# Fifteen more tiles turned by VectorE in 32x32 blocks and carried by small transfers, in a two-block transformer kernel in float32

## What is computed

```python
def first_block(x, mem, ...):
    for i in range(2):
        if i == 1:
            sk1, sk2, sv = shared_kv(x, kv_norm, w_kv, k_norm, cos, sin)
        u = rms_norm(x, mix_norm[i]) @ w_in[i]
        ...                                   # pooling (i = 0) or differential attention (i = 1)
        mem_out = memory_cross_attention(mem_q, mem, ...)
        x = x + concatenate([token_out, mem_out]) @ w_out[i]
        x = x + squared_relu_mlp(rms_norm(x, ffn_norm[i]), w_ff1[i], w_ff2[i])
    return x
# second block
#   u = rms_norm(x) @ w_in_2, split in eight parts; recurrence and attention on them
#   merged = sigmoid(m1) * (lru @ w_proj_a) + sigmoid(m2) * (att @ w_proj_b)
#   x = x + rms_norm(merged @ w_out_2) * norm_post
```

## Time and profile before

| | us |
|---|---|
| median of 3 runs | 3058.63 |
| lowest and highest | 3057.3, 3058.84 |
| the profiled execution, its own time | 3060.36 |
| its span | 3058.6 |
| PE busy in it | 3002.9 |
| ACT, DVE, POOL busy | 1504.9, 1793.7, 239.2 |

### The profile page before, as it was taken

One profiled execution on the slowest core, in us unless ns is written; L12 is line 12 of the kernel. 1 busy time (PEld: TensorE's weight loads), 2 busy tenths in 40 slices (PEclk: granted clock), 3 DMA queues, 4 the chain that ended last, 5 costly groups with the idle time before them and its releaser, 6 DMA issues.

```text
span 3058.6 us, 37252 instructions
## 1 busy us (share of the span) xinstructions
PE 3002.9 (98%) x13708; PEld 2484.1 (81%) x13708; DVE 1793.7 (59%) x2382; ACT 1504.9 (49%) x2019; POOL 239.2 (8%) x465
## 2 busy tenths in 40 slices
PE   8999999999999999999999999999999999999998
PEld 7877888888888778778888888888888888787886
DVE  6535655555455776866545555555546567786554
ACT  6534434444344555654434344444445547785433
POOL 0000302112030000001203021120000000010000
PEclk9999999999999999999999999999999999999999
DMA  7535666666675555546666666665665555666664
GB/s 258 183 113 178 214 200 199 205 192 210 188 227 187 165 167 156 166 146 197 202 201 204 200 198 206 192 206 206 203 199 186 157 166 172 192 205 202 225 240 152
DMA packets 313433, 586.12 MB, mean 192 GB/s; under 512 B 24784, under 2 KB 49744, under 8 KB 312528
## 3 DMA queue, kind: packets, MB, share of 16 engines
q1 hardware_dynamic: 293248, 541.13, 56.4%
q0 software_dynamic: 19472, 42.24, 4.3%
q10 hardware_dynamic: 576, 0.94, 0.1%
HBM read 561.15 MB, written 10.49 MB: 187 GB/s over the span
## 4 chain that ended last, share of the span: by engine, by line
PE 84%; DVE 8%; ACT 6%; issue 2%; DMA 0%; ACTq 0%; DVEq 0%
PE acc L1741 26%; PE acc L1743 26%; PE acc L1742 26%; ACT whi L909 2%; DVE wlo L1222 2%; PE tp L1759 1%; DVE wlo L1217 1%; ACT prob L1132 1%; PE sd L1822 1%; PE sd L1804 1%; PE sd L1910 1%; ACT qk L1140 0%; ACT whi L912 0%; ACT L1132 0%; PE sd L1900 0%
## 5 line engine op out<-in xcount | busy, mean ns | idle before, releaser
L1741 PE MATMUL acc<-whi,set_hi 128*128 128x512 f32 x4096 | 1618.6, 395 | 24.4 <-DVE wlo L1222 15.5
L1743 PE MATMUL acc<-whi,set_lo 128*128 128x512 f32 x4096 | 1597.4, 390 | 0.0
L1742 PE MATMUL acc<-wlo,set_hi 128*128 128x512 f32 x4096 | 1596.5, 390 | 0.0
L1222 DVE TENSOR_TENSOR wlo<-raw,whi 128x1024 fp32r<-128x1024 f32 x944 | 1131.9, 1221 | 683.9 <-ACT whi L909 682.9
L909 ACT ACTIVATE whi<-raw 128x1024 fp32r<-128x1024 f32 x944 | 975.3, 1057 | 764.2 <-PE acc L1743 622.1
L1741 PEld LDWEIGHTS acc<-whi,set_hi 128*128 128x128 f32 x4096 | 770.6, 188 | 197.6 <-DVE wlo L1222 24.6
L1743 PEld LDWEIGHTS acc<-whi,set_lo 128*128 128x128 f32 x4096 | 770.1, 188 | 163.0
L1742 PEld LDWEIGHTS acc<-wlo,set_hi 128*128 128x128 f32 x4096 | 771.0, 188 | 155.0
L875 POOL DMA_DIRECT2D u<-u x384 | 188.2, 498 | 1509.2 <-DVE u L1336 1474.1
L1217 DVE SCALAR_TENSOR_TENSOR wlo<-raw,par,whi 128x512 fp32r<-128x512 f32 x160 | 111.9, 748 | 52.6 <-ACT whi L912 51.8
L912 ACT ACTIVATE whi<-raw,par 128x512 fp32r<-128x512 f32 x160 | 103.8, 715 | 18.0 <-DMA raw<-in_w_kv 8.1
(11 more groups left out here) (233 smaller groups left out, 1240.5 us busy)
## 6 DMA issues: line engine op xcount, KB each, us to landing
raw<-in_w_ff SPq DMA_DIRECT2D x512, 512.0 KB, 4.6
raw<-in_w_in SPq DMA_DIRECT2D x248, 512.0 KB, 4.2
raw<-in_w_out SPq DMA_DIRECT2D x96, 512.0 KB, 4.3
raw<-in_w_mem_kv SPq DMA_DIRECT2D x32, 512.0 KB, 4.6
raw<-in_w_proj_a SPq DMA_DIRECT2D x32, 512.0 KB, 4.4
raw<-in_w_proj_b SPq DMA_DIRECT2D x32, 512.0 KB, 5.5
u<-u POOLq DMA_DIRECT2D x384, 32.0 KB, 4.9
raw<-in_w_kv SPq DMA_DIRECT2D x48, 256.0 KB, 3.3
```

Source lines behind the costliest of these rows:

```text
L1222: V.tensor_tensor(wlo[:, c], raw[:, c], whi[:, c].bitcast(f32), ALU.subtract).then_inc(w_lo, 1)
L1741: T.matmul(o, h[:, tok], whi[:, c], start=first, stop=False)
L1742: T.matmul(o, h[:, tok], wlo[:, c], start=False, stop=False)
L1743: ins = T.matmul(o, l[:, tok], whi[:, c], start=False, stop=last)
```

## The change

Fifteen tiles go from `tail` to `turned`: the first three of the four in both output projections, at the end of both feed-forward parts, and of the merged product in the second block. The fourth of each stays with PE.

- `turned`, `turn` and `shuffle` take a `room`: "u0" and "u1" are two pairs of areas in `u`, "kv" a pair in `kv`. (The plan's other names of rooms are not used by any tile.)
- POOL waits, ahead of the transfers of every turned tile, until all transfers of the earlier ones have landed.
- Where a norm's weights belong to the tile (`ffn0`, `ffn1`, and `pre` at the end of the second feed-forward part), ACT multiplies the turned tile by them in place, in four instructions on 128x256, waits for the last of them (`link`), and then copies it to `set_hi` in one of 128x1024. At the end of the first feed-forward part and in the merged product there are no weights, and the copy alone stands.
- The groups that read these tiles wait for the second tile before slab 0, for the third before slab 4, for the fourth before slab 6 (`fed_late`). The first group of the last product still waits for three tiles before slab 0.

```diff
-    def turned(self, slab_turn, slab_split, source, dst, kt, gain=None):
+    def turned(self, slab_turn, slab_split, source, dst, kt, gain=None, room="u0"):
...
+    def fed_late(self, g):
+
+        for k, left in ((0, 2), (NSLAB - 4, 1), (NSLAB - 2, 0)):
+            self.groups[g].need[k] = [("tail_lo", self.tails - left)]
...
             e = sc.end(g)
             sc.epilogue(g, "add", GW * i)
             sc.at("act", e + 1, "x_stat", rst_ffn, i, g)
-            sc.tail(e + 3, e + 5, ("x", i, g), dst, 4 * i, f"ffn{layer}")
+            if i < 3:
+                sc.turned(e + 1, e + 9, ("x", i, g), dst, 4 * i, f"ffn{layer}", room=f"u{i % 2}")
+            else:
+                sc.tail(e + 3, e + 5, ("x", i, g), dst, 4 * i, f"ffn{layer}")
...
             sc.epilogue(g, "add", GW * i)
             sc.at("act", S * (g + 1) + 1, "x_stat", next_rst, i, g)
             fs.append(g)
         for i, g in enumerate(fs):
-            sc.tail(S * (g + 1) + 3, S * (g + 1) + 5, ("x", i, g), a, 4 * i, next_gain)
+            if i < 3:
+                sc.turned(S * (g + 1) + 1, S * (g + 2) + 1, ("x", i, g), a, 4 * i, next_gain)
+            else:
+                sc.tail(S * (g + 1) + 3, S * (g + 1) + 5, ("x", i, g), a, 4 * i, next_gain)
...
         sc.epilogue(b, "proj_b", sc.tails)
-        sc.tail(S * (b + 1) + 3, S * (b + 1) + 5, ("out", b), 0, 4 * i)
+        if i < 3:
+            sc.turned(S * (b + 1) + 1, S * (b + 2) + 1, ("out", b), 0, 4 * i, room="kv")
+        else:
+            sc.tail(S * (b + 1) + 3, S * (b + 1) + 5, ("out", b), 0, 4 * i)
...
-            def shuffle(t, n):
-
+            def shuffle(t, n, room):
+
+                blocks, turned = rooms[room]
+                if n:
+                    pool.wait_ge(sm["shuffled"], 256 * n)
                 pool.wait_ge(sm["tail_tp"], at(t + 1))
...
+                    elif gain is None:
+                        ins = A_(in_blocks(sets[dst][0][:, TOK * kt:TOK * (kt + 4)]), tp, ACT.Copy)
+                    else:
+                        z = rooms[lent[2]][1].rearrange("p (q n c) -> p n q c", q=4, n=4)
+                        for j in range(4):
+                            ins = A_(z[:, j], z[:, j], ACT.Copy, scale=gain_of(gain, kt + j))
+                        link(ins)
+                        ins = A_(in_blocks(sets[dst][0][:, TOK * kt:TOK * (kt + 4)]), tp, ACT.Copy)
```

More of the change, by code:

```diff
@@ L168, in turned @@
         self.turns += 1
[L169 to L172, removed]
+        self.at("dve", slab_turn, "turn", t, source, room)
+        self.at("pool", slab_turn, "shuffle", t, n, room)
+        self.at("act", slab_split, "tail", t, dst, kt, gain, ("turned", n, room))
+        self.at("dve", slab_split, "tail", t, dst, kt, gain, ("turned", n, room))
         return t
@@ L293, in ffn @@
         first = sc.group(f"w_ff1{layer}", 0, 0, a)
-        sc.groups[first].need[0] = [("tail_lo", sc.tails - 1)]
-        sc.groups[first].need[S - 2] = [("tail_lo", sc.tails)]
+        sc.fed_late(first)
         sc.loops[first + 1] = dict(layer=layer, tail0=sc.tails, staged0=sc.staged, turn0=sc.turns, rst=rst, a=a, z=z)
@@ L315, in ffn @@
             if i == 0:
-                for k, left in ((0, 2), (S - 4, 1), (S - 2, 0)):
-                    sc.groups[g].need[k] = [("tail_lo", sc.tails - left)]
+                sc.fed_late(g)
             sc.epilogue(g, "add", GW * i)
@@ L524, in build @@
         addend = kv[:, LB * UTW + 8 * P:LB * UTW + 8 * P + 2 * TOK]
-        blocks, turned = u[:, 0:TB * GW], u[:, TB * GW:2 * TB * GW]
+        w = TB * GW
+        rooms = {"u0": (u[:, 0:w], u[:, w:2 * w]), "u1": (u[:, 2 * w:3 * w], u[:, 3 * w:4 * w]),
+                 "values": (kv[:, 2 * w:3 * w], kv[:, 5 * w:6 * w]), "kv": (kv[:, 4 * w:5 * w], kv[:, 5 * w:6 * w]),
+                 "x": (x[:, 2 * w:3 * w], x[:, 3 * w:4 * w])}
         gt = x
@@ L1305, in tail @@
                 dve.wait_ge(sm["tail_hi"], at(t + 1))
+                if isinstance(lent, tuple) and dst == "ut":
+                    for j in (2, 3):
+                        o = ut_tiles(kt + j, 1)[:, 0].rearrange("p (b q t) -> p b q t", b=TB, q=4)
+                        ins = V.tensor_copy(o, tp[:, TB * j:TB * (j + 1)])
+                    ins.then_inc(sm["tail_lo"], 1)
+                    return
+                if isinstance(lent, tuple) and dst == "gt":
+                    V.tensor_copy(in_blocks(gt[:, TOK * (kt + 2):TOK * (kt + 4)]), tp[:, 2 * TB:4 * TB])\
+                        .then_inc(sm["tail_lo"], 1)
+                    return
                 if dst == "ut":
```

57 lines of the change are left out of this document (33 added, 24 removed).

## The result

| | before | after |
|---|---|---|
| median, us | 3058.74 (6 runs) | 3070.99 (6 runs) |
| lowest and highest | 3056.66, 3060.97 | 3069.4, 3072.44 |
| profiled execution, span | 3058.6 | 3069.0 |
| its own time | 3060.36 | 3070.8 |

The ratio is 1.0041, 95% interval 1.0031 to 1.0051: slower, by more than 0.2%. The forecast was 3063.9: the time lies inside its range, but 7 us above it, and the outcome is not the one that the forecast held the likeliest (a change too small to tell, 0.48) but the second (slower, 0.37). The two profiled executions are 10.4 us apart; before's was 1.6 above its median, which makes up the rest.

The account below looks back on a forecast made before the run. The prediction took PE as the bound, busy 3002.9 of 3058.6 us. Its terms, -13.6 - 1.4 + 4.0 + 1.0 + 7.2 + 2.8 + 5.3 = +5.3 us, added to the median 3058.63 gave 3063.9; range 3047 to 3074.

Parts of the forecast that it names:

- A PE turn costs 0.91 us: Each of the 15 turns taken from PE saves 0.91 us, 13.6 us in all, all on the path.
- The room of 0.45 us: Behind a residual add, `lo` of the third slab ends at +4.99 us and PE wants it at +5.44.
- The first rival: Waits at the feed-forward ends are hidden: 3043.6 us if the pair's wait is too, otherwise 3049; chance 0.14.
- "4.0" and "7.2" at the ends: PE waits behind second and third adds: 2.0 us twice at the first feed-forward end, 3.6 twice at the second.
- The last boundary: Behind the fourth add of the second feed-forward end, `lo` of the third slab and the chain come 2.8 us later.
- Scalings 1.6 us: ACT's four pieces multiplying a turned tile by the norm's weights take 1.6 us, 2.0 kept for the range.
- The woven pair, 5.3: Layer 1's projection: PE waits 5.3 us because the second tile's transfers land late; ends 0 and 8.
- Inner parts 0: The inner parts of the feed-forward, between the new places: no change in time, 0 us.
- Layer 0, -1.4: Layer 0's projection: softplus starts earlier, PE's wait falls from 1.7 to 0.3 us, gaining 1.4; ends 0 and 1.7.
- The projections 0: Output projections: transfers land at +16.3 us, ahead of ACT's tail some 17.4 after the group's former end; no cost.
- Merged product 0: Second block's merged product: `lo` of the third slab ends at +5.17 us, PE wants it at +5.44; no wait.
- Collisions: Rival: transfers and weight loads collide, or POOL's instructions come late, in the new places; 10 us more, 3074; chance 0.14.

Follow-up runs that it names:

- tails_first: The changed kernel with the tail at both feed-forward ends named ahead of the next group's add and squares: 3049.55 us.
- ffn_ends_alone: The changed kernel with only the six tiles at the feed-forward ends turned, the nine of projections and merged product back on PE: 3072.71 us.
- no_scalings: The changed kernel without the multiplication by the norm's weights for the turned tiles at the second feed-forward end, copies kept: 3062.46 us.
- double_scalings: The changed kernel with the three turned tiles at the second feed-forward end multiplied by the norm's weights twice: 3076.33 us.
- change_shifted: The changed kernel with 51 and 86 added waits on things long done, so both inner loops lie in PE's list as before the change: 3069.60 us.
- before_shifted: The kernel before the change with 157 added waits on things long done between the two inner loops, moving the second loop's place in PE's list: 3071.62 us.

## Why the prediction was right and wrong

- **A PE turn costs 0.91 us**: right. Groups without one are 21.76 us apart at the ends and in the projections, and merged adds 2880.57 - 2837.05 = 43.52, forecast 43.6:

```profile
2837.05 1.22 DVE L1326 TENSOR_TENSOR stage_b<-acc,mkv 128x1024 f32<-128x1024 f32 x1 [3.06 <-PE acc L1790]
...
2880.57 1.23 DVE L1326 TENSOR_TENSOR stage_b<-acc,mkv 128x1024 f32<-128x1024 f32 x1 [3.06 <-PE acc L1790]
```

- **The room of 0.45 us, and the tail behind the add as the place of the loss**: right, and shown by tails_first. The first rival (hidden waits) is out.
- **"4.0" and "7.2" at the ends**: the step that failed. The forecast made PE's loss equal to the wait, 2.0 and 3.6 each. The waits measured 1.78 and 3.52, and stops of these lengths cost 2.1 and 3.8 us with the clock up (the second by ffn_ends_alone), so this part was right. The losses were 3.66 and 2.08, and 5.4 twice, because the clock was slow behind three of the four, at 1.6 us each. Nothing in the forecast priced what follows a wait. The last boundary is of the same kind: its wait grew by 1.8 and not by 2.8, a slow stretch followed, and together they cost 3.4. In all this is 5.8 us of the miss.
- **Scalings 1.6 us**: 1.70; no_scalings and double_scalings show them on the path in full.
- **The woven pair, 5.3**: mechanism right, size off. The landings came 2.8 us after the last issue for the first tile and 4.8 for the second, not 5.4 for each. The stretch cost 2.9. The Trainium skill's 2.0 us for such a transfer ("DMA: Bandwidth & Descriptors", "Anatomy of one DMA — SWDGE (gpsimd) path") would have made the wait nothing. The trace agrees for neither tile, with 2.8 and 4.8 us, and the profile's median from issue to landing is 5.0.
- **Inner parts 0**: they cost 2.3. Taking instructions out of PE's list moved the loops' code, and their four returns loaded blocks again (119 transfers on q8 for 84); change_shifted puts the code back and the 2.3 are gone from its trace. The forecast looked at what engines do, not at where their code lies.
- **Layer 0, -1.4**: the size is right, the account only in part. PE's longest wait there fell from 1.70 to 0.97 us, not to 0.3; but before the change there was a second one, of 0.37, in the same group, and it went too. The term is also loose: in the other runs with these tiles turned the gain there was 0.7 to 2.0 us.
- **The projections 0**: right but for the pair, with a slip that changes nothing: the 16.3 us there are six slabs of 2.72, not five.
- **Merged product 0**: right. **Collisions**: none at the feed-forward ends, as tails_first shows, and at the new places of the projections ACT waits up to 3 us for loads while PE's waits stay at 1 us and less, the pair aside. A late POOL, the other half of that rival, is seen in two variants of the change and not in the change.
- The errors of both signs add up to the miss of 5.1 by the profiled executions (10.4 - 5.3): 5.8 + 2.3 - 2.4 - 0.5, with 0.1 of rounding. That the miss is no larger is luck in part: the pair's overpriced wait hid 2.4 us of it. The upper end of the range came from collisions, pieces and a late POOL, none of which is what cost the time.

## What to carry to other kernels

When work is moved to a quieter engine, its place in that engine's list matters more than its length: the same instructions ahead of the epilogue cost next to nothing, behind it some 20 us for six tiles. Price a wait of TensorE by what follows it too. And when a measured difference is a few tenths of a per cent in a kernel with loops, look at PE's idle time for "issue" at the loops' returns and at the instruction queue on the page before believing any account by engines: here moving code alone was worth 12.4 us, as much as the change.

## What the runs showed of the hardware

- TensorE's granted clock was at 1.2 GHz for some 2.5 to 6 us behind most stops of 3.5 us and more (eight matmuls 0.43 us apart behind 3.52, 12 and 6 behind 5.25), which cost 1.4 to 2.6 us on top of the stop itself. Behind 1.78 us it fell in 4 of 12 places, behind the stops of 2.46 and 2.60 us in 8 of 12 traces each. A stop after which the clock stayed up cost 0.3 us more than the wait that the profile gives (2.08 for 1.78).
- The return of a loop of 1,630 PE instructions cost nothing, 0.3 to 1.3 us, or 5.4 to 6.8 us, by where the loop began in PE's list. Modulo 256: in the first loop nothing at 44 and 45, the middle figures at 250; in the second nothing at 117, 152, 161 and 165, the middle figures at 15, the high ones at 66. The pages have 84 transfers on q8 where no return costs anything, 102 or 103 where those of one loop do and 119 or 120 where those of both do: some nine blocks for a return, whether it costs 0.3 us or 6. The Trainium skill, "Runtime: NRT & Kernel Launch", section "Instruction fetch mechanics", says that PE holds 2048 instructions in blocks of 256, and that a taken branch out of what is held stalls. The traces agree with the blocks (16 KB each) and with the stall (3.73 us). That a loop shorter than what is held is loaded again at some positions is what before_shifted shows.
- Sixteen transfers of 32 KB between partitions take POOL 7.8 us to issue and had landed 2.8 and 4.8 us after the last issue at the pair, 5.4 in the inner part.
